# Down projection of a conv FFN: 44 steps of a plain split product, or seven half-size products

## The reference

```python
h_lat = _modulate(_rms_norm(x, norm2[i]), m_lat[3], m_lat[4])
x = x + m_lat[5] * _conv_ffn(h_lat, w_up[i], ffn_conv[i], ffn_conv_b[i], w_down[i], True)
...
return _rms_norm(x, final_norm)

def _conv_ffn(h, w_up, conv_w, conv_b, w_down, on_grid):
    u = h @ w_up
    u = _conv_grid_3x3(u, conv_w, conv_b) if on_grid else ...
    a, v = jnp.split(u, 2, axis=-1)
    return (jax.nn.silu(a) * v) @ w_down
```

## Time and profile before

| | |
|---|---|
| time, median of 3 runs | 1649.36 us (1646.6 to 1652.43) |
| span of the profiled execution | 1648.8 us |
| PE busy | 1605.8 us, 97% |
| DVE busy | 1228.9 us, 75% |
| ACT busy | 560.9 us, 34% |
| POOL busy | 450.6 us, 27% |
| down projection on PE | 1392.84 to 1640.2 us |

### The profile page before, as it was taken

One profiled execution on the slowest core, in us unless ns is written; L12 is line 12 of the kernel. 1 busy time (PEld: TensorE's weight loads), 2 busy tenths in 40 slices (PEclk: granted clock), 3 DMA queues, 4 the chain that ended last, 5 costly groups with the idle time before them and its releaser, 6 DMA issues.

```text
span 1648.8 us, 20721 instructions
## 1 busy us (share of the span) xinstructions
PE 1605.8 (97%) x8142; PEld 1197.5 (73%) x8142; DVE 1228.9 (75%) x1761; ACT 560.9 (34%) x892; POOL 450.6 (27%) x435
## 2 busy tenths in 40 slices
PE   7999999999999989999999999999999999999997
PEld 2545555995599955656588888888888887887886
DVE  5587887699766679888876599889888898434435
ACT  2544343552343322222744322222222223223332
POOL 5001101221233256565134433233333333100000
PEclk9999999999999999999999999999999999999999
DMA  9276454864398540000523211111111112522332
GB/s 348 82 263 222 132 192 166 255 159 108 105 292 232 167 153 26 14 26 14 205 96 122 65 51 52 51 50 40 52 51 51 45 46 85 196 90 89 115 130 88
DMA packets 201389, 194.79 MB, mean 118 GB/s; under 512 B 40117, under 2 KB 155135, under 8 KB 201164
## 3 DMA queue, kind: packets, MB, share of 16 engines
q1 hardware_dynamic: 194608, 190.00, 36.1%
q10 hardware_dynamic: 6396, 3.20, 0.7%
...
## 4 chain that ended last, share of the span: by engine, by line
PE 56%; DVE 5%; ACT 1%; issue 1%; POOL 1%; DMA 0%; ACTq 0%; DVEq 0%; POOLq 0%
PE PS L2159 10%; PE PS L2163 10%; PE PS L2161 10%; PE PS L2198 5%; PE PS L2200 5%; PE PS L2202 5%; PE PS L2017 4%; PE PS L2032 2%; DVE Qbd L2460 2%; PE PS L2119 1%; PE PS L2121 1%; PE PS L2120 1%; PE PS L2054 1%; DVE AT L2476 1%; DVE Ex L2441 1%
## 5 line engine op out<-in xcount | busy, mean ns | idle before, releaser
L2631 DVE SCALAR_TENSOR_TENSOR acc<-PS,fcol,acc 128x945 f32<-128x945 f32 (+2 forms) x176 | 215.1, 1222 | 29.2 <-ACT acc L2290 23.6
L2631 DVE SCALAR_TENSOR_TENSOR act<-PS,fcol,act 128x945 f32<-128x945 f32 (+2 forms) x176 | 215.1, 1222 | 21.7 <-ACT act L2290 16.2
L2159 PE MATMUL PS<-h2hi,whi 128*128 128x512 f32 x704 | 219.5, 389 | 0.0
L2161 PE MATMUL PS<-h2lo,whi 128*128 128x512 f32 x704 | 219.3, 389 | 0.0
L2163 PE MATMUL PS<-h2hi,wlo 128*128 128x512 f32 x704 | 219.3, 389 | 0.0
L425 PE MATMUL PS<-hT,wq 128*128 128x512 f32 (+1 forms) x432 | 163.1, 537 | 0.0
L1969 POOL TENSOR_TENSOR wlo<-wu,whi 128x1024 fp32r<-128x1024 f32 x44 | 106.4, 2422 | 207.3 <-ACT whi L2283 206.9
L2161 PEld LDWEIGHTS PS<-h2lo,whi 128*128 128x128 f32 x704 | 132.1, 188 | 27.4
L2163 PEld LDWEIGHTS PS<-h2hi,wlo 128*128 128x128 f32 x704 | 132.1, 188 | 27.4
L2159 PEld LDWEIGHTS PS<-h2hi,whi 128*128 128x128 f32 x704 | 132.1, 188 | 27.4
L2642 DVE TENSOR_TENSOR wrlo<-wr,wrhi 128x1024 fp32r<-128x1024 f32 x41 | 50.2, 1224 | 128.4 <-ACT wrhi L2380 128.4
...
## 6 DMA issues: line engine op xcount, KB each, us to landing
...
```

What stands on the lines that cost most here:

```text
L2159: pe.matmul(PS[:, b + half, :], whi[k][u][:, kk, :], h2hi[:, 4 * half:4 * half + 4, kk, :], start=(kk == 0), stop=False)
L2161: pe.matmul(PS[:, b + half, :], whi[k][u][:, kk, :], h2lo[:, 4 * half:4 * half + 4, kk, :], start=False, stop=False)
L2631: tp = v.scalar_tensor_tensor(out=t_[:, r0:r1, c0:c1], in0=up[:, r0 + dr:r1 + dr, c0 + dc:c1 + dc], scalar=tap_col(j, k, f), in1=t_[:, r0: ...
```

## The change

The product A·B (A the activations, B the weights) is cut into blocks, A into two token halves times two feature halves of 11 x 128 (KH = 11), B into two feature halves times two column halves of 512. Instead of eight block products seven are made, in the variant of Strassen's scheme that has these terms:

- S1 = A21 + A22, S2 = S1 - A11, S3 = A22 - S2, S4 = A12 - S2, made by POOL, 128x512 at a time: `sums_of_a` (two operations per j), `s3_of`, `s4_of`. S1, S2 and S4 are written over `act`.
- T3 = B22 - B12, T2 = B11 + T3 (`t3_of`, `t2_of`: DVE); T1 = B12 - B11 (`t1_of`: POOL, one operation), T4 = B21 - T2 (`t4_of`: POOL, two operations).
- The products in order, 11 steps each, are listed in PRODUCTS7. A step is now 128 features x 512 tokens x 512 columns: 12 matmuls of the same shape, three in a row to one bank. There are 77 steps. A product uses four banks, products alternate between banks 0 to 3 and 4 to 7, and some products are accumulated onto the one before last.
- The sums of products (y10, y01, y11, y00, each 128x4x512) are made between the products by DVE and ACT, and the gate and the addition of x for them by POOL (`gate_and_add`), tile by tile.

The buffers are again four sets of raw, high and low parts, each now 128x512, and a step's load still waits for the step four before it. The low parts of the first six steps are POOL's. For products 2, 4 and 6 (A_LOW7) the activations' low part is POOL's (`a_low`); the weights' low part of every later step and the activations' low part in the other products are DVE's. The last four steps are run token tile by token tile. The final norm works on half rows: of its sums of squares one part is made per column half.

The core of the diff, with the added lines only; the order of the queues is that of the code (the first lines after each "..." that use `sp`, `g`, `pe`, `a`, `v` are SP, POOL, PE, ACT, DVE):

```diff
 NB7 = 4
+NR7 = 3
...
+KH = FT // 2
+PRODUCTS7 = ("A11 B11", "S2 T2", "A12 B21", "S3 T3", "S1 T1", "A22 T4", "S4 B22")
+STEPS7 = len(PRODUCTS7) * KH
+TAIL7 = 4
+HEAD7 = 6
...
+def at7(s):
+    return s // KH, s % KH, s % NB7
...
+def tok_half(f, i):
+    return act[f][:, i * HALF:(i + 1) * HALF]
+def a_of(s):
+    p, j, u = at7(s)
+    if p == 3:
+        return as7[u][:, :]
+    return tok_half(j + KH if p in (2, 5, 6) else j, 1 if p in (4, 5) else 0)
+def b_of(s):
+    p, j, u = at7(s)
+    return t3[j][:, :] if p == 3 else raw7[u][:, :]
...
+A_LOW7 = (2, 4, 6)
...
+        def second(n, src):
+            if n >= NR7:
+                m, j = n - NR7, (n - NR7) % KH
+                if m < KH:
+                    sp.wait_ge(s_7t3, j + 1)
+                elif m < 2 * KH:
+                    sp.wait_ge(s_7t, T1_FROM + j + 1)
+                else:
+                    sp.wait_ge(s_7t, T4_FROM + 2 * j + 1)
+            elif n:
+                sp.wait_ge(s_6g, FT)
+            sp.dma_start(r2[n % NR7][:, :], src).then_inc(s_7y[n % NR7], 16)
+        def t3_in(j):
+            second(j, b_block(0, 1, j))
+            sp.dma_start(t3[j][:, :], b_block(1, 1, j)).then_inc(s_7y[j % NR7], 16)
+        def step_in(s):
+            p, j, u = at7(s)
+            if p == 1 and j + NR7 < KH:
+                t3_in(j + NR7)
+            if p in (4, 5):
+                second((p - 3) * KH + j, b_block(0, 0, j))
+            if p == 3:
+                return
+            if s >= NB7:
+                sp.wait_ge(s_7f, s - NB7 + 1)
+            k, c = ((0, 0), (0, 0), (1, 0), None, (0, 1), (1, 0), (1, 1))[p]
+            sp.dma_start(raw7[u][:, :], b_block(k, c, j)).then_inc(s_7w[u], 16)
...
+        for s in range(NB7, STEPS7):
+            if s == 8:
+                for j in range(NR7):
+                    t3_in(j)
+            if s == 4 * KH:
+                sp.wait_ge(s_7g, Y01_DONE)
+                x1_quarter(1, 0)
+            if s == 5 * KH + 3:
+                sp.wait_ge(s_7g, Y10_DONE)
+                x1_quarter(0, 0)
+            if s == 6 * KH + 4:
+                sp.wait_ge(s_7t, T4_FROM + 2 * KH)
+                sp.dma_start(fng[:, :], final_norm.rearrange("(o n) -> o n", o=1).to_broadcast([P, D])).then_inc(s_7n, 16)
+                sp.wait_ge(s_7g, Y00_DONE)
+                x1_quarter(1, 1)
+            step_in(s)
...
+        def low7(s):
+            u = s % NB7
+            g.wait_ge(s_7h, s + 1)
+            g.tensor_tensor(rlo7[u][:, :], raw7[u][:, :], rhi7[u][:, :], ALU.subtract)
+            g.wait_ge(s_7ah, s + 1)
+            g.tensor_tensor(alo7[u][:, :], a_of(s), ahi7[u][:, :], ALU.subtract).then_inc(s_7lp, 1)
+        def sums_of_a(j):
+            g.wait_ge(s_6g, KH + j + 1)
+            g.tensor_tensor(tok_half(j, 1), tok_half(j, 1), tok_half(KH + j, 1), ALU.add).then_inc(s_7s, 1)
+            g.wait_ge(s_7s, 2 * j + 1)
+            if j < HEAD7:
+                g.wait_ge(s_7lp, j + 1)
+            else:
+                g.wait_ge(s_7lv, j - HEAD7 + 1)
+            g.tensor_tensor(tok_half(j, 0), tok_half(j, 1), tok_half(j, 0), ALU.subtract).then_inc(s_7s, 1)
+        def a_low(s):
+            g.wait_ge(s_7ah, s + 1)
+            g.tensor_tensor(alo7[s % NB7][:, :], a_of(s), ahi7[s % NB7][:, :], ALU.subtract).then_inc(s_7la, 1)
+        def s4_of(j):
+            g.wait_ge(s_7la, j + 1)
+            g.wait_ge(s_7s, 2 * j + 2)
+            g.tensor_tensor(tok_half(KH + j, 0), tok_half(KH + j, 0), tok_half(j, 0), ALU.subtract).then_inc(s_7s, 1)
+        def s3_of(j):
+            s = 3 * KH + j
+            g.wait_ge(s_7f, s - NB7 + 1)
+            g.tensor_tensor(as7[s % NB7][:, :], tok_half(KH + j, 1), tok_half(j, 0), ALU.subtract).then_inc(s_7s, 1)
+        def second_in(n):
+            g.wait_ge(s_7y[n % NR7], second_loads7(n))
+        def t1_of(j):
+            s = 4 * KH + j
+            g.wait_ge(s_7w[s % NB7], raw_loads7(s))
+            second_in(KH + j)
+            g.tensor_tensor(raw7[s % NB7][:, :], raw7[s % NB7][:, :], r2[(KH + j) % NR7][:, :], ALU.subtract).then_inc(s_7t, 1)
+        def t4_of(j):
+            s = 5 * KH + j
+            g.wait_ge(s_7w[s % NB7], raw_loads7(s))
+            second_in(2 * KH + j)
+            g.tensor_tensor(raw7[s % NB7][:, :], raw7[s % NB7][:, :], r2[(2 * KH + j) % NR7][:, :], ALU.subtract).then_inc(s_7t, 1)
+            g.wait_ge(s_7t, T4_FROM + 2 * j + 1)
+            g.tensor_tensor(raw7[s % NB7][:, :], raw7[s % NB7][:, :], t3[j][:, :], ALU.subtract).then_inc(s_7t, 1)
+        def gate_and_add(y, c, t, ready, n, done):
+            if t == 0:
+                g.wait_ge(s_7c, 16)
+                g.wait_ge(s_7q, ready)
+                g.wait_ge(s_7x, 16 * n)
+            g.tensor_tensor(y[:, t, :], y[:, t, :], gbc2[:, c * HALF:(c + 1) * HALF], ALU.mult).then_inc(s_7g, 1)
+            g.wait_ge(s_7g, done + 2 * t + 1)
+            g.tensor_tensor(y[:, t, :], y[:, t, :], xq[:, t, :], ALU.add).then_inc(s_7g, 1)
+        for s in range(HEAD7):
+            low7(s)
         gated(FT - 1)
+        for j in range(KH):
+            sums_of_a(j)
+        for j in range(KH):
+            a_low(2 * KH + j)
+            if j:
+                s4_of(j - 1)
+        s4_of(KH - 1)
+        for j in range(KH):
+            s3_of(j)
+            if 3 <= j < 3 + TT:
+                gate_and_add(y01, 1, j - 3, 1, 1, 0)
+        for j in range(KH):
+            t1_of(j)
+            if j:
+                a_low(4 * KH + j - 1)
+            if 6 <= j < 6 + TT:
+                gate_and_add(y10, 0, j - 6, 3, 2, Y01_DONE)
+        a_low(5 * KH - 1)
+        for j in range(KH):
+            t4_of(j)
+        g.wait_ge(s_7q, 2)
+        g.wait_ge(s_7x, 48)
+        for t in range(TT):
+            a_low(6 * KH + t)
+            g.tensor_tensor(y00[:, t, :], y00[:, t, :], xq[:, t, :], ALU.add).then_inc(s_7g, 1)
+        for j in range(TT, KH):
+            a_low(6 * KH + j)
+        for t in range(TT):
+            gate_and_add(y11, 1, t, 4, 4, Y00_DONE)
+        g.wait_ge(s_7n, 16)
+        for t in range(TT):
+            g.wait_ge(s_7sq, t + 1)
+            g.tensor_tensor(y00[:, t, :], y00[:, t, :], fng[:, 0:HALF], ALU.mult).then_inc(s_7fg, 1)
...
+        def part(s, t):
+            p, j, u = at7(s)
+            b = 4 * (p % 2) + t
+            fresh = p in (0, 1, 4) and j == 0
             tok = slice(t * P, (t + 1) * P)
+            pe.matmul(PS[:, b, :], ahi7[u][:, tok], rhi7[u][:, :], start=fresh, stop=False, skip_group_check=True)
+            pe.matmul(PS[:, b, :], ahi7[u][:, tok], rlo7[u][:, :], start=False, stop=False, skip_group_check=True)
+            return pe.matmul(PS[:, b, :], alo7[u][:, tok], rhi7[u][:, :], start=False, stop=(j == KH - 1), skip_group_check=True)
+        def banks_free(p, t):
+            if p < 2:
+                pe.wait_ge(s_6v[t // 2], FT - 1 + p)
+            elif p == 2:
+                pe.wait_ge(s_7p1, 1)
+            else:
+                pe.wait_ge(s_7q, p - 2)
+        for s in range(STEPS7 - TAIL7):
+            p, j, u = at7(s)
+            ready(s)
             for t in range(TT):
...
+        for s in range(3, STEPS7):
+            high7(s)
+            if s == KH + 3:
+                a.wait_ge(s_7p, 1)
+                a.activation(y10[:, :, :], PS[:, 0:TT, :], ACT.Copy).then_inc(s_7p1, 1)
+            if s == 6 * KH + 5:
+                a.wait_ge(s_7t, T4_FROM + 2 * KH)
+                for t in range(TT):
+                    a.wait_ge(s_7g, Y10_DONE + t + 1)
+                    square(t, t, y00, fsa)
+        for t in range(TT, NL):
+            a.wait_ge(s_7g, Y00_DONE + 2 * (t - TT) + 2)
+            square(t, t, y11, fsa)
+        a.wait_ge(s_7e, 1)
+        for t in range(TT, NL):
+            square(NL + t - TT, t, y10, fsb)
+            root(t)
+        def scaled_y00(t):
+            a.wait_ge(s_7i, TT + t + 1)
+            a.wait_ge(s_7fg, t + 1)
+            a.activation(y00[:, t, :], y00[:, t, :], ACT.Copy, scale=frs[:, t:t + 1]).then_inc(s_7o2, 1)
         for t in range(TT):
+            a.wait_ge(s_7e, 2 + t)
+            square(NL + TT + t, t, y01, fsb)
+            root(t)
+            if t:
+                scaled_y00(t - 1)
+        scaled_y00(TT - 1)
...
+        def low7(s):
+            u = s % NB7
+            v.wait_ge(s_7h, s + 1)
+            bl = v.tensor_tensor(rlo7[u][:, :], b_of(s), rhi7[u][:, :], ALU.subtract)
+            if s // KH in A_LOW7:
+                bl.then_inc(s_7lv, 1)
+                return
+            v.wait_ge(s_7ah, s + 1)
+            v.tensor_tensor(alo7[u][:, :], a_of(s), ahi7[u][:, :], ALU.subtract).then_inc(s_7lv, 1)
+        def t3_of(j):
+            v.wait_ge(s_7y[j % NR7], second_loads7(j))
+            v.tensor_tensor(t3[j][:, :], t3[j][:, :], r2[j % NR7][:, :], ALU.subtract).then_inc(s_7t3, 1)
+        def t2_of(j):
+            s = KH + j
+            v.wait_ge(s_7t3, j + 1)
+            v.wait_ge(s_7w[s % NB7], raw_loads7(s))
```

(37 more changed lines are left out.)

291 lines of the change are left out of this document (143 added, 148 removed).

## The result

The changed kernel takes 1696.3 us (median of 4 runs, 1695.4 to 1697.2) against 1650.1 for the kernel before (4 runs beside it): the ratio is 1.028, with a 95% interval from 1.026 to 1.029. It is 2.8% slower, at 17 us above the forecast of 1679 and inside the range of 1650 to 1698. The profiled execution has a span of 1693.6 us where the sum gave 1678.

What follows compares the result with a forecast made beforehand. PE's stream of matmuls bounds the kernel now; the change saves 30 us there but adds 53 us ahead of the tail, mostly from POOL and DVE. Last steps at 1644.2 plus 34 of tail give span 1678, median 1679; range 1650 to 1698.

Steps and rivals of the forecast that it cites:

- The exchange at 1.67 us: Wherever POOL and DVE both read SBUF: one POOL operation and one DVE operation of 0.68 alternate, 1.67 us per pair.
- where 17.6 + 2.5 stood: Products 0 and 1: PE 17.6 us late at step 12 from POOL and DVE alternating, plus 2.5 for PE's lower clock.
- over 90% there: Product 1: the prediction is wrong if PE is over 90% busy in it.
- where 4.5 stood: Products 2 and 3: product 2 about 1 us late, product 3's gate steps 7 us too many, half absorbed; +4.5.
- the three steps made ahead: Product 3: three steps prepared early were to take half of the 7 us too many in its four gate steps.
- where 12.3 stood: Product 4: four gate steps of 5.3 us, six of 3.05 limited by POOL's order; 42.2 against 29.9, +12.3.
- where 8 stood: Product 5: two POOL and two DVE operations per step, ten steps of 3.34 us, 1.7 at the start; +8.
- where 2 + 5.9 stood: Product 6: +2 for SP's wait for y00 and two DVE operations; +5.9 for the stall before the last four steps.
- where 34 stood: Tail: POOL's y11 gates, then ACT and DVE rather than PE set the end; 34 us with the last store.
- the 45 named among the signs: Profile after: one PE gap of 5 to 6 us some 45 us before the end.
- rival (c): PE's clock falls with each gap and starved steps cost double: 1694 to 1715 us; chance 0.12.
- (a): The prediction's own sum, with POOL and DVE alternating and POOL's load as the bound: 1662 to 1694 us; chance 0.60.

Runs made afterwards that it cites:

- The blanks: Changed kernel with POOL's operations after its first twelve replaced by memsets that read nothing, in three lengths (0.76, 0.92, 1.09 us): 1641.6, 1649.6 and 1657.9 us.
- the third kernel with blanks: Changed kernel with each POOL operation after its first twelve replaced by eighteen memsets of 29 columns, 1.09 us together: 1657.9 us, ratio 1.004.

## Why the prediction was right, and what it mis-sized

**The sign and the cause** were right. PE lost its 132 matmuls at the same spacing, and the low parts came late because DVE and POOL exclude each other. The blanks show it: with POOL writing instead of reading DVE's `rlo` takes 704 ns in the mean instead of 1061, and 28 to 30 us go. The exchange at 1.67 us, worked out from operations of 0.3 us, measured 1.68. The Trainium skill (SBUF — State Buffer, section on who interferes with whom) says that such a DVE operation contends with a GpSimd one that reads SBUF and not with one that only writes; the trace agrees, with 0.68 us beside 118 memsets. The same page of the Trainium skill, in the section on SBUF's two separate sides that the prediction cites, has the other engine fully blocked for the whole instruction. By the whole lengths of the earlier trace rows that is 1.98 a pair; 1.68 was measured, so the trace agrees in kind, with 0.3 less at the hand-over.

**Products 0 and 1: 23.9 us over the unhindered 59.8, where 17.6 + 2.5 stood.** The turns were counted rightly: 14 us leave with the sums. The step that the sum left out is SP's queue, held by the wait for `gated(21)`, with DVE idle for 7 us. Taking that away gave only 2.7 us in a profile and 1 us in the medians. It counts for more once the turns are gone: in the third kernel with blanks the step before step 8 still takes 5.8 us (1413.7 to 1419.6) and step 8 at the lower clock 4.4, about 5 of the 9.8 us that it has over the unhindered time. The other 5 lie in steps 2 to 5 and around step 11, and stay open. The place was also put wrongly: PE's gaps lie in product 0 and in the first step of product 1, and product 1 itself has PE busy for 32.7 of 33.5 us. The text had said that over 90% there would speak against it; it doesn't, since its own sum has the lateness end at step 12, and step 12 began at 1447.3 where 1443.0 was worked out. The 2.5 us set aside for the lower clock were not spent: step 8, mostly at a clock of 0.50, lasted 5.04 us and step 9, at 1.00, 5.06, each as long as three turns of DVE.

**Products 2 and 3: 10.5 us where 4.5 stood.** This is the largest miss. Product 2 is 3.3 over, of which 2.7 are its last step (1503.0 to 1508.4), PE waiting for S3's way through ACT and DVE; 1 was reckoned. Product 3 is 7.2 over, of which 3.5 were to be saved by "the three steps made ahead". There were none, as S3 comes after the whole of product 2 in POOL's order, and the turns made POOL late with it: the first three steps took 3.4 us each. Of the four steps with a gate only the first took the 4.5 reckoned (4.6), the others 3.4.

**Product 4: 15.9 us where 12.3 stood.** The steps with a gate took 5.5 us each (1561.5 to 1583.5), where 4 x 1.2 + 0.5 = 5.3 was reckoned. The others took 2.8 to 3.0, as worked out, with 4.1 and 4.9 at two of them. The 4.9 is the last step, and the 2.2 us too many in it are PE's wait for step 55's operands, from T4 on, which the sum had under product 5 with 1.7.

**Product 5: 7.1 us where 8 stood**, a figure that is right in part by luck. Ten steps of 3.34 us were reckoned, and only three took 3.4. Five took 2.7 to 2.9, and longer ones made up for it: step 57 with 4.3 and step 62 with 3.8, after POOL had been idle for 0.93 and 1.41 us for the loads of steps 58 and 63, and step 58 with 4.8, beside DVE's read of the banks (128x2048, 2.28 us from 1601.69). What each of these waits costs was not tried.

**Product 6 to the last four steps: 12.2 us where 2 + 5.9 stood.** The stall was sized rightly: 8.1 us from step 72's start to step 73's, 5.4 over a step, with PE idle for 5.2. The wait of SP for y00's addition was named, and priced at up to 2 us together with two operations of DVE. It cost 5.3 us before step 70 and 1.5 in it, because the transfer went out 5.5 us late (step 66 had ended at 1631.0), took 5.29 us beside the x quarter, where 3.4 had been taken as the most that a load could need, and the clock had dropped by then. Moving the wait gave back 6.6 us in the profile and 8 in the medians.

**The tail: 34.1 where 34 stood**, in the predicted order. But the stall ahead of it is not a cost of its own: with one more step of PE's work in the hole nothing changed. That gap of PE lies 34 us before the end, as the sum has it, and not the 45 named among the signs.

**The clock** was not the rival (c), although the 1696 us lie in (c)'s range of 1694 to 1715 and just above the 1662 to 1694 that (a) gave itself. After the gap of 4.8 us it was 0.50, the level of 1.2 GHz, and matmuls were back at their spacing of 0.23 us from 1425.8; windows of the changed kernel:

```profile
1420.00:1422.00 2.00, 0.49 (x1) 0.49 (x2) 2.00 (x2) 1.11 (x3) 1.92 (x2) 0.50 0.00 0
1422.00:1424.00 2.00, 2.00 (x6) 1.54 (x6) 2.00 (x2) 0.00 (x0) 2.00 (x2) 0.50 0.00 0
```

From 1442 to 1446 it was 0.50 again, and that cost nothing, since step 12 began at 1447.3, the moment that DVE's low part of it ended. In products 2, 3 and 5, where PE waits for a fraction of many steps, it stayed at 1.00, so the starved steps did not cost double. Before the last four steps it fell again, in a gap of 5.2 us. **POOL** was to be busy for over 85% of the stage; it is 224 of 302 us, 74%, with the idle time in product 1 and at the end.

**Together** the terms were low by 3.8, 6.0, 3.6 and 4.3 us and high by 0.9: 16.8 us. PE reached the stage 1.3 us sooner (1391.5 for 1392.84), which is chance, and 1678 + 16.8 - 1.3 is the measured span of 1693.6 within 0.1.
